# The expert half of a hybrid decoder layer: gather per four experts, scatter from rounded halves, sums that start from the residual

## The reference, cut to what matters

```
def moe(u, router_w, router_b, w_gate, w_up, w_down):      # u: 256 x 1024
    scores = sigmoid(u @ router_w)                          # 16 experts in 4 groups
    ... best group by its two highest scores + router_b, then the two best experts in it
    weights = top_s / sum(top_s);  combine = one_hot(top_idx) * weights   # 256 x 16
    out = 0
    for e in range(16):                                     # d_ff 512
        he = silu(u @ w_gate[e]) * (u @ w_up[e])
        out = out + combine[:, e:e+1] * (he @ w_down[e])
    return out

# in the layer:
    x = x + gt_a * mixer(modulate(rms_norm(x, g_mix), sh_a, sc_a))
    u = modulate(rms_norm(x, g_ffn), sh_f, sc_f)
    x = x + gt_f * moe(u)
return rms_norm(x, g_final)
```

## Time and profile before

| | |
|---|---|
| median of three runs | 666.17 us |
| span of the profiled execution | 663.3 us |
| what lies around the span (median less span) | 2.9 us |
| TensorE busy | 630.7 us (95%) |
| VectorE busy | 332.2 us (50%) |
| ScalarE busy | 243.2 us (37%) |
| bytes moved | 184.76 MB, mean 279 GB/s |

### The profile page before, as it was taken

The page is one execution under the profiler, slowest core; times in us unless marked ns, Lnnn a source line. Parts: engine busy times, 40 slices in busy tenths (PEclk is TensorE's granted clock), DMA queues, the critical chain, the costliest instruction groups (busy, mean ns, idle before and its releaser), DMA issues.

```text
span 663.3 us, 9100 instructions
## 1 busy us (share of the span) xinstructions
PE 630.7 (95%) x3817; PEld 465.4 (70%) x3817; DVE 332.2 (50%) x546; ACT 243.2 (37%) x357; POOL 5.6 (1%) x13
## 2 busy tenths in 40 slices
PE   4697999999999999999999999999999999999993
PEld 4697988999998888999998864444453535444440
DVE  3876976857679878684556551112121211111125
ACT  3415647354453476546424552021121302111121
POOL 3000000000000000000000000000000000000000
PEclk9797999999999999999999979999999999999998
DMA  9994553886678964465647796999999999999701
GB/s 316 361 379 159 191 191 127 298 274 224 221 253 271 358 223 172 136 237 191 216 166 254 260 375 229 385 389 400 387 400 387 401 387 401 387 401 387 280 1 65
DMA packets 86313, 184.76 MB, mean 279 GB/s; under 512 B 5401, under 2 KB 5505, under 8 KB 86273
## 3 DMA queue, kind: packets, MB, share of 16 engines
q1 hardware_dynamic: 83746, 184.06, 76.9%
q10 hardware_dynamic: 2528, 0.16, 0.3%
HBM read 183.16 MB, written 1.05 MB: 278 GB/s over the span
## 4 chain that ended last, share of the span: by engine, by line
PE 92%; DVE 4%; DMA 2%; issue 1%; ACT 0%; SPq 0%; DVEq 0%; ACTq 0%
PE ps L1218 30%; PE ps L1226 15%; PE ps L1464 8%; PE ps L1443 8%; PE ps L1444 8%; PE ps L1427 5%; PE ps L1420 5%; PE ps L1454 2%; DMA raw<-in_ada_w_dram 2%; PE ps L1289 1%; PE ps L1328 1%; PE ps L1313 1%; PE ps L1376 1%; PE ps L1275 1%; PE ps L1301 1%
## 5 line engine op out<-in xcount | busy, mean ns | idle before, releaser
L1218 PE MATMUL ps<-u_hi,hi 128*128 128x256 f32 x448 | 131.0, 292 | 9.3 <-DVE u_lo L782 9.3
L722 DVE TENSOR_TENSOR lo<-raw,hi 128x2048 fp32r<-128x2048 f32 x52 | 118.7, 2288 | 35.6 <-ACT hi L505 35.3
L1218 PE MATMUL ps<-u_lo,hi 128*128 128x256 f32 x448 | 128.8, 287 | 0.0
L1218 PE MATMUL ps<-u_hi,lo 128*128 128x256 f32 x448 | 128.7, 287 | 0.0
L505 ACT CAST hi<-raw 128x2048 fp32r<-128x2048 f32 x52 | 98.8, 1908 | 50.0 <-PE ps L1218 24.7
L1443 PE MATMUL ps<-ring,xe_t 128*64 128x512 f32 x256 | 111.6, 594 | 0.0
L1444 PE MATMUL ps<-ring,xe_t 128*64 128x512 f32 x256 | 111.5, 594 | 0.0
L1218 PEld LDWEIGHTS ps<-u_hi,hi 128*128 128x128 f32 x448 | 88.1, 197 | 9.6 <-DVE u_lo L782 9.5
L1218 PEld LDWEIGHTS ps<-u_lo,hi 128*128 128x128 f32 x448 | 88.2, 197 | 0.1
L1218 PEld LDWEIGHTS ps<-u_hi,lo 128*128 128x128 f32 x448 | 87.9, 196 | 0.0
L1106 DVE SCALAR_TENSOR_TENSOR he<-ps,scat,sg 64x512 f32<-64x512 f32 x16 | 12.0, 750 | 115.7 <-ACT sg L689 115.7
(11 more groups left out here) (282 smaller groups left out, 851.9 us busy)
## 6 DMA issues: line engine op xcount, KB each, us to landing
raw<-in_w_in_dram SPq DMA_DIRECT2D x42, 1024.0 KB, 5.4
ring<-in_w_gate_e_dram SPq DMA_DIRECT2D x32, 1024.0 KB, 12.0
ring<-in_w_up_e_dram SPq DMA_DIRECT2D x32, 1024.0 KB, 14.1
ring<-in_w_down_e_dram SPq DMA_DIRECT2D x32, 1024.0 KB, 14.3
raw<-in_ada_w_dram SPq DMA_DIRECT2D x24, 1024.0 KB, 5.8
raw<-in_w_branch_m_dram SPq DMA_DIRECT2D x4, 1024.0 KB, 5.3
raw<-in_w_out_dram SPq DMA_DIRECT2D x4, 1024.0 KB, 5.5
raw<-in_w_branch_a_dram SPq DMA_DIRECT2D x2, 1024.0 KB, 6.1
```

What stands on the lines that cost most here:

```text
L722: V.tensor_tensor(lo[b % RING][:], src[:], hi[b % RING][:].bitcast(F32), ALU.subtract).then_inc(lo_ready, 1)
L1218: ins = mm(dst, w[:, k, cols], x[:, k0 + k, :], start=(first and c % 2 == 0 and k == 0 and n == 0), stop=(end and k == KB - 1 and n == 2), ...
```

## The change

It rewrites the expert half:

- **Gather per four experts.** The one-hot matrix has 256 columns (four experts) and is built by two VectorE instructions. The normed residual is split into `xg_hi` (rounded, ScalarE) and `xg_lo` (the rest, GpSimd), and `gather_part` runs 32 fp32r matmuls with 256 columns for four experts. ScalarE and VectorE share the way to `xe_t`: parts 0 and 2, and 1 and 3.
- **Both experts of a pair in one bank.** `gate_or_up` does gate of both experts side by side in `ps[4]`, then up of both in `ps[5]`; Silu and the product run once over 128 partitions; `turn_he` is four full transposes; `down` does both experts side by side in `ps[6]` and `ps[7]`.
- **Scatter in two fp32r parts.** VectorE multiplies the output by the gate `mod[:, 3]` on its way out of PSUM (`gate_y`), ScalarE rounds it (`y_hi_e`), VectorE takes the rest (`y_lo_e`), and `scatter` adds both with fp32r matmuls: eight for a pair.
- **Sums from the residual.** The four banks start as the residual (an identity matrix times `x_res`) in place of zeros, so that they hold the new residual after the last scatter. ScalarE squares them straight from PSUM, VectorE scales them straight from PSUM.
- **Ring freed in twos.** The ring has 16 slots of 1 MiB. A group is one half (of the contraction) of one matrix for both experts of a pair, 2 MiB; one semaphore, `group_used`, counts groups, and SyncE refills two slots after each. The first eight groups are loaded ahead as before, the last three of them one mixer block apart.
- The new helpers wait and then do one thing: `round_y` copies `y_e` to `y_hi_e` (128x1024), `gate_silu` takes Silu of `ps[4]` to `sg` (128x512), `turn_out` copies `ps[6]` to `he_t` (128x512), `gate_y` is two products of 128x512 out of `ps[6]` and `ps[7]`, `split_y` one difference of 128x1024, `take_slots` copies the turned one-hot matrix to `scat`, `weigh` is one product of 128x512. For a pair TensorE does the two gate halves, `turn_slots`, the two up halves, half of the scatter of the pair before, `turn_he`, the other half of that scatter, after an odd pair the four `gather_part` of the next four experts, and the two down halves.
- The pairs are written out straight, without a loop; only the repeat for over 64 tokens is a loop.

```diff
-        ring = [at(f"ring{i}", k, [P, KT * FF]) for i, k in enumerate((80, 140, 104, 0, 16, 32, 48, 64))]
+        ring = [at(f"ring{i}", k, [P, KB * FF]) for i, k in enumerate(
+            (80, 88, 140, 148, 104, 112, 0, 8, 16, 24, 40, 64, 48, 72, 32, 56))]
...
+            for g in range(5, 8):
+                sp.wait_ge(block_done, NBLK - 7 + g)
+                load_group(g)
...
+            for g in range(RSLOTS // 2, PAIRS * NPART):
+                sp.wait_ge(group_used, g - RSLOTS // 2 + 1)
+                load_group(g)
@@ GpSimd
+            for t in range(TT):
+                after(pool, f"x_hat{t}")
+                nc.gpsimd.tensor_tensor(xg_lo[:, t, :], x_hat[:, t, :], xg_hi[:, t, :].bitcast(F32), ALU.subtract
+                                        ).then_inc(lo_split, 1)
@@ ScalarE
             for t in range(TT):
-                ins = A_(x_hat[:, t, :], x_res[:, t, :], ACT.Copy, scale=st[:, 14 + t:15 + t])
+                A_(xg_hi[:, t, :], x_res[:, t, :], ACT.Copy, scale=st[:, 14 + t:15 + t])
+                event(A_(x_hat[:, t, :], x_res[:, t, :], ACT.Copy, scale=st[:, 14 + t:15 + t]), f"x_hat{t}")
...
+            for p in range(PAIRS):
+                if p:
+                    round_y(p - 1)
+                gate_silu(p)
+                turn_out(p)
+                if p % 2 and p < PAIRS - 1:
+                    for kb in (0, 2):
+                        act.wait_ge(gathered, 4 * (p // 2 + 1) + kb + 1)
+                        fill_xe(kb, 4 * SLOTS, 4)
...
             for t in range(TT):
-                after(act, f"x2_t{t}")
-                event(A_(x_hat[:, t, :], x_res[:, t, :], ACT.Square, accum_out=st[:, 16 + t:17 + t]), f"x2_ss{t}")
+                act.wait_ge(moe_done, t + 1)
+                for h in range(2):
+                    ins = A_(squares[:], ps[2 * t + h][:], ACT.Square, scale=1.0 / 32.0,
+                             accum_out=st[:, 16 + 2 * t + h:17 + 2 * t + h])
@@ VectorE
+            for p in range(PAIRS):
+                if p:
+                    dve.wait_ge(group_used, p * NPART)
+                    gate_y()
+                    dve.wait_ge(y_hi_ready, p)
+                    split_y()
+                dve.wait_ge(slots_turned, p + 1)
+                take_slots(p % 2)
+                if p % 2 and p < PAIRS - 1:
+                    build_onehot(p // 2 + 1)
+                dve.wait_ge(scat_ready, p + 1)
+                dve.wait_ge(sg_ready, p + 1)
+                dve.wait_ge(group_used, p * NPART + 4)
+                weigh(p % 2)
...
@@ TensorE
-            for b in range(3):
-                mm(ps[b][:], zeros[:, 0:P], zeros[:], start=True, stop=False, skip_group_check=True)
+            start_sums(0, 0)
+            start_sums(0, 1)
+            start_sums(1, 0)
...
+            def gather_part(kb, cols, bank):
+                for kk in (2 * kb, 2 * kb + 1):
+                    dst = ps[bank][:, (kk % 2) * T:(kk % 2) * T + cols]
+                    for n, (x, t) in enumerate(((xg_hi, 0), (xg_lo, 0), (xg_hi, 1), (xg_lo, 1))):
+                        ins = mm(dst, x[:, t, kk * P:(kk + 1) * P], onehot[:, t, 0:cols],
+                                 start=(kk % 2 == 0 and n == 0), stop=(n == 3), skip_group_check=True)
+                ins.then_inc(gathered, 1)
+            def gate_or_up(bank, half, slots, col):
+                for k in range(KB):
+                    kk = KB * half + k
+                    for s in range(2):
+                        w = ring[slots[s]][:].rearrange("p (k n) -> p k n", k=KB)
+                        ins = mm(ps[bank][64 * s:64 * s + 64, :], xe_t[:, kk, col + s * SLOTS:col + (s + 1) * SLOTS], w[:, k, :],
+                                 start=(kk == 0), stop=(kk == KT - 1))
+                ins.then_inc(group_used, 1)
...
+            pe.wait_ge(lo_split, TT)
+            pe.wait_ge(onehot_ready, 1)
+            gather_part(0, 4 * SLOTS, 7)
+            gather_part(1, 4 * SLOTS, 5)
+            pe.wait_ge(xe_act, 1)
+            gather_part(2, 4 * SLOTS, 7)
+            pe.wait_ge(xe_dve, 1)
+            gather_part(3, 4 * SLOTS, 5)
+            for p in range(PAIRS):
+...
+                if p:
+                    pe.wait_ge(y_split, p)
+                    pe.wait_ge(scat_ready, p)
+                    scatter((p - 1) % 2, 0)
+                pe.wait_ge(he_ready, p + 1)
+                turn_he()
+                if p:
+                    scatter((p - 1) % 2, 1)
+                if p % 2 and p < PAIRS - 1:
+...
+                pe.wait_ge(scat_ready, p + 1)
+                pe.wait_ge(he_t_ready, p + 1)
+                for half in range(2):
+                    down(half, group_slots(p * NPART + 4 + half))
```

More of the change, by code:

```diff
@@ L103 @@
 POS = {item: n for n, item in enumerate(STREAM)}
-CHUNKS = 8
-PAIR_CHUNKS = (("gate", 0), ("up", 0), ("gate", 1), ("up", 1), ("down", 0), ("down", 1))
-BODY = 8
+QUADS = NE // 4
+PAIRS = NE // 2
+RSLOTS = 16
+PARTS = [(matrix, half) for matrix in ("gate", "up", "down") for half in range(2)]
+NPART = len(PARTS)
 def build(nc, A, out):
@@ L214, in build @@
         w_pair = small("w_pair", [P, TT, 2])
+        w_slot = small("w_slot", [P, 2])
         many = small("many", [P, 2])
@@ L415, in _, with load @@
             matrices = {"gate": A["w_gate_e"][0], "up": A["w_up_e"][0], "down": A["w_down_e"][0]}
[L416 to L421, removed]
+            def load(slot, p, part, e):
+                matrix, half = PARTS[part]
+                w = matrices[matrix][(2 * p + e) % NE].rearrange("(k p) n -> p k n", p=P)
@@ L422, in load_half @@
                 k = w.shape[1] // 2
[L423 to L440, removed]
-                            sp.wait_ge(used, n)
-                            load_half(CHUNKS + j, h)
-                            load_half(CHUNKS + j + 1, h)
+                sp.dma_start(ring[slot][:].rearrange("p (k n) -> p k n", k=k), w[:, half * k:(half + 1) * k, :]
+                             ).then_inc(ring_loaded[slot], 16)
@@ new lines, in gate_y, with split_y, take_slots @@
+            def gate_y():
+                for h in range(2):
+                    ins = V.tensor_tensor(y_e[:, h * NB:(h + 1) * NB], ps[6 + h][:], mod[:, 3, h * NB:(h + 1) * NB], ALU.mult)
+                    ins.then_inc(y_out, 1)
+            def split_y():
+                V.tensor_tensor(y_lo_e[:], y_e[:], y_hi_e[:].bitcast(F32), ALU.subtract).then_inc(y_split, 1)
+            def take_slots(side):
+                V.tensor_copy(scat[side][:], ps[7][:, 0:T])
+                for s in range(2):
+                    rows_s = slice(64 * s, 64 * s + 64)
+                    ins = V.tensor_copy(w_slot[rows_s, side:side + 1], ps[7][rows_s, T + s:T + s + 1])
+                ins.then_inc(scat_ready, 1)
@@ L1123, in _, with weigh @@
+            def weigh(side):
+                V.scalar_tensor_tensor(out=he[:], in0=ps[5][:], scalar=w_slot[:, side:side + 1], in1=sg[:],
+                                       op0=ALU.mult, op1=ALU.mult).then_inc(he_ready, 1)
             dve.wait_ge(consts_ready, 6)
@@ new lines, in down @@
+            def down(half, slots):
+                for k in range(2):
+                    kk = 2 * half + k
+                    for h in range(2):
+                        for s in range(2):
+                            w = ring[slots[s]][:].rearrange("p (k n) -> p k n", k=2)
+                            ins = mm(ps[6 + h][64 * s:64 * s + 64, :], he_t[:, kk, s * SLOTS:(s + 1) * SLOTS],
+                                     w[:, k, h * NB:(h + 1) * NB], start=(kk == 0), stop=(kk == FF // P - 1))
+                ins.then_inc(group_used, 1)
@@ L1485, in _, with group_slots @@
-            after(pe, "x_hat")
-            with pe.Fori(0, NE // BODY) as i:
-                for q in range(BODY // 2):
-                    work_pair(i, q)
+                    for y in (y_hi_e, y_lo_e):
+                        ins = mm(ps[2 * t + h][:], scat[side][:, t * P:(t + 1) * P], y[:, h * NB:(h + 1) * NB],
+                                 start=False, stop=False, skip_group_check=True)
+                return ins
+            def group_slots(g):
+                slots = [(2 * g + e) % RSLOTS for e in range(2)]
+                for e in range(2):
+                    pe.wait_ge(ring_loaded[slots[e]], 16 * ((2 * g + e) // RSLOTS + 1))
+                return slots
```

356 lines of the change are left out of this document (186 added, 170 removed).

## The result

The changed kernel takes **650.16 us** (median of four runs, 649.75 to 650.91), the kernel before 666.23 us in the runs beside it. The ratio is 0.9764, with a 95% interval of 0.9746 to 0.9783. The profiled execution took 649.75 us, with a span of 647.8 us, so 1.9 us lie around it. In every execution on record, of any of the kernels, it is 1.7 to 2.0 us; the 2.9 of the table before takes the span of one execution from the median of three others, so that execution itself took some 665.2 us (an estimate: 663.3 plus 1.9).

The account below looks back on a forecast made before the run. TensorE bounds the kernel before, the weight stream the changed one: first gate 404.0, last data 624.2, span 642.2, plus 2.9 around it, gives 645 us against 666.17 (2.0 front, some 18.3 wait, 0.8 end saved). Range 640 to 654.

Parts of the forecast that it names:

- The bound: Expert half: TensorE decides before; after the change the weight stream at 394 GB/s does, from the seventh or eighth pair.
- 16.8 MB at 90 GB/s: Ring: the head start of loaded weights, used up after some 187 us, when TensorE begins to wait.
- rival (c): Weight stream: slower, at 358 GB/s, so 666 us and no change; chance 0.02.
- A pair on TensorE: Expert half: TensorE's work for two experts falls from 31.03 to 26.0 us.
- The front: Before the expert half: first gate at 404.0, 2.0 us earlier, with GpSimd's differences hidden and 1.7 us to spare.
- The end: After the last data at 624.2: TensorE done at 627.8, then product, split, scatter and scaling to a span of 642.2 us.
- The sum: Whole kernel: span 642.2 us plus 2.9 around it, 645 us; 21 us saved.
- the likeliest case: Whole kernel: the forecast with small costs of GpSimd and the clock, 641 to 650 us; chance 0.75.
- rival (a): Last pairs: TensorE's clock falls in waits on the ring, at most 5.0 us, so 650 us; beyond the forecast, chance 0.11.
- (b): Weight stream: not at its limit, a faster TensorE draws more, so 630 us; chance 0.07.
- (d): Straight pair code: instruction fetches wait under full queues, 14.3 us each, 673 us from the third, 702 with five; chance 0.03.
- (e): Gate, up and down: two tiles with different weights in one bank don't run side by side, 797 us; chance 0.01.

Follow-up runs that it names:

- e3: The changed kernel with the loads of groups 16 to 19 bringing only half their rows, 4 MiB less of 96: 639.08 us.
- e4: The changed kernel with the four turns of `he` done five times for each pair, as added TensorE work: 651.46 us.
- e2: The kernel before, with two added GpSimd differences of 128x1024 whose result nobody uses: 670.84 us, ratio 1.0072.
- e8: The changed kernel with each GpSimd difference cut into eight pieces of 128 columns: 648.02 us.
- e1: The changed kernel without GpSimd's differences and ScalarE's two `x_hat` tiles; VectorE makes `xg_lo` itself in pieces: 646.20 us.
- e7: e1 with two more float32 matmuls on TensorE around the wait for the router's picks, to keep its clock up: 645.13 us.
- e5: The changed kernel with its gather back in plain float32, without rounded half or GpSimd difference: 646.59 us.
- e6: The changed kernel with its scatter in plain float32 from `y_e`; rounding and difference still done, but nothing waits for them: 649.52 us.
- e10: e7 with the first group of the ring freed in two halves and the last group loaded and awaited in two halves: 643.58 us.

## Why the prediction was right, and where it was off

- **The bound.** Right: the stream decides from the last pairs on. First refill at 413.57 to last data at 630.33 are 216.8 us; the forecast was 216.6. e3 and e4 show it from both sides. The waits began earlier than the sum had it: at 540, in the sixth pair, 130 us after the first gate, where 16.8 MB at 90 GB/s were to last 187 us. Two things can account for it, by argument only: the stream began 3.6 us after the first gate and then had to come up, and what is under way at any time (some 5 MiB by the forecast's own count) is not yet there to be used; for the end it made no difference, as the stream's own length sets it. The 358 GB/s that the Trainium skill gives in "DMA: Bandwidth & Descriptors", Specifications, did not appear: 394 again, and rival (c) is out.
- **A pair on TensorE.** 26.3 us against 26.0. The gather takes 4.23 us, some 3.8 of them matmuls and 0.4 a wait for a fill that lies mostly under the next part; the turn of `he` is 0.47 against 0.5, half a scatter 0.92 to 1.14 against 0.92. Waits on the ring 15.9 us against "some 15".
- **The front.** Wrong, and this is the whole of the difference: first gate at 409.9, not 404.0. The step that failed is the one that let GpSimd's differences run "hidden with 1.7 us to spare". Their length was well put (2.34 each, forecast 2.6). It asked only whether they end in time. What was missing is that they aren't free while they run: VectorE's instructions with two SBUF operands wait for them, 3.8 us in the router's chain (e2 and e8; e1 fits). The Trainium skill, "GPSIMD Engine Reference", section 1. Specifications, names this contention, for VectorE instructions with two SBUF inputs; the trace agrees, with 2.30 for 0.26 us, and I hadn't weighed it. On top of this TensorE's clock was low, which the sum had at full: the rank sums took 2.32 us in place of 1.31, behind the wait of 5.31 (e1, with a shorter wait, has 1.30 back), and the first 16 gather matmuls 3.5 us in place of 1.9. The second part isn't GpSimd's doing: e1 has it too, and e7 shows it gone. These are 6.4 us; the profiled execution reached the router 0.5 earlier, which leaves 5.9.
- **The end.** Nearly right: 3.8 us from last data to TensorE's end (3.56 forecast), then 13.7 (14.4). I had the first half of the last scatter at low clock, 1.84 us; it took 1.21. This is chance: behind the same wait of 3.7 us it took 1.21 at a granted clock of 1.00 here and in e1, and 2.09 at 0.50 in e5 and e7.
- **The sum.** Span: +5.9 for the front, +0.2 for the stream, +0.2 and -0.7 at the end is 647.8 in place of 642.2. Around the span it was 1.9, and the forecast's 2.9 was a reading of two different executions. So 650.16 lies inside the range of 640 to 654 but just beyond the likeliest case, 641 to 650, where only rival (a) had been given a chance, and (a) did not happen. That the range still held it is partly luck: its upper end was there for longer GpSimd work and for a low clock in the waits on the ring, not for a router that GpSimd holds up. Of the 21 us forecast, 16 came.
- **Rivals.** (a) is out: the clock was 1.00 through all waits on the ring, up to 1.9 us each. The rule of the Trainium skill, "TensorE: Matmul & The Clock Gate", section on HAM oscillation, on bursts shorter than the waits between them had no case on the ring, as each burst there was 3.5 us or longer. (b), (d) and (e) are out: 394 GB/s, no idle time of the matmuls without a releaser above 0.7 us, gate and up in 14.06 us (7.02 + 7.04) for a pair.
- **Where the gain came from.** From the first gate to the last down it was 242.1 us before and 224.2 after, of which 15.9 are waits on the ring. So 33.8 us of work were taken from TensorE; 15.9 came back as waits, 3.9 were lost at the front, and 14.0 are left, with 1.5 from the end. Each of the fp32r parts alone could be left out (e5, e6); what the pairing of experts gives by itself no run shows.

## What to carry to other kernels

When two resources are close, work out when the second one ends before pricing the work taken from the first: here anything over 22 / 8 = 2.8 us a pair turned into waits on the ring. Work given to an engine that is "free" must be priced by what it blocks, not only by whether it ends in time; an independent instruction on GpSimd beside a chain of small VectorE instructions cost 5.0 us in one kernel (e2) and some 4 in the other (e1). Once a stream decides, its start counts one for one when all its refills move with it (e1: first refill 4.8 us earlier, last data 4.7), but not when only the first does (e10: 1.9 and 0.65). What follows its last byte counts until TensorE's own tail is longer than the stream's, which came after 0.5 us.

## What the runs showed of the hardware that was not expected

- A VectorE instruction with two SBUF operands (128x16, 0.13 us) that starts under a GpSimd tensor_tensor of 128x1024 (2.34 us) ends when that one ends: the pair at 393.04 ends at 395.34, and the first of GpSimd's two (half of 4.68 from 392.85) at 395.19. The reductions with one SBUF input between the pairs kept their length (0.19 for 0.18). With pieces of 128 columns the wait is 0.1 to 0.5 us, and some instructions with one SBUF tensor and a per-partition scalar grew too (0.58 for 0.37).
- TensorE's clock stayed at full speed in waits of up to 1.9 us between bursts of 3.5 us, over 90 us; in the front it was at 0.50 after two waits of 1.6 us with small matmuls between them (e1), and at 1.00 when these waits were 0.7 us (e7).
- Behind one and the same wait of 3.7 us at the end the clock was at 1.00 in some executions (changed kernel, e1) and at 0.50 in others (e5, e7).
